# Two transformer blocks on one core: the mLSTM heads, the out products and one norm in another order

## The reference

```python
def mlstm_mixer(x, norm_g, w_in, b_gates, h_norm_g, w_out):
    u = rmsnorm(x, norm_g) @ w_in
    q, k, v, o, gi, gf = jnp.split(u, M_SPLITS, axis=-1)      # 4 heads, dqk 128, dv 256
    ...
    h = mlstm_chunkwise(q, k, v, i_pre, f_pre)
    h = rmsnorm(h, h_norm_g.reshape(M_HEADS, M_DV))...        # a mean of squares per head
    h = h * jax.nn.sigmoid(o.astype(jnp.float32))             # the output gate
    return h.astype(x.dtype) @ w_out

# per head: s = (q k^T) * exp(dmat - m);  num = s v;  den = sum(s)
#           h = num / max(|den|, exp(-m))
# moba_mixer: 8 heads of 128; causal softmax over the 256 tokens; then o @ w_o
# conv_ffn:   rmsnorm, @ w_up (5632 wide), 3-tap causal convolution, silu(gate) * val, @ w_down
```

## Time and profile before

| what | us |
|---|---|
| median of 3 runs (lowest, highest) | 1027.2 (1026.81, 1027.39) |
| the profiled execution: its own time | 1025.42 |
| its span, first to last instruction | 1023.6 |
| PE busy (share of the span) | 987.5 (96%) |
| DVE busy | 632.9 (62%) |
| ACT busy | 274.1 (27%) |

### The profile page before, as it was taken

One profiled execution on the slowest core, in us unless ns is written; L12 is line 12 of the kernel. 1 busy time (PEld: TensorE's weight loads), 2 busy tenths in 40 slices (PEclk: granted clock), 3 DMA queues, 4 the chain that ended last, 5 costly groups with the idle time before them and its releaser, 6 DMA issues.

```text
span 1023.6 us, 15183 instructions
## 1 busy us (share of the span) xinstructions
PE 987.5 (96%) x5811; PEld 882.9 (86%) x5811; DVE 632.9 (62%) x1400; ACT 274.1 (27%) x602; POOL 1.1 (0%) x8
## 2 busy tenths in 40 slices
PE   6999899999999999999999999999999989999987
PEld 5788588999999988888899999999888878888876
DVE  2302437878778571254287867875799951799843
ACT  1111301121121122244022111112433553623651
POOL 0000000000000000000000000000000000000000
PEclk9999999999999999999999999999999999999999
DMA  8991036577577292450537767754733035443001
GB/s 254 354 354 48 1 124 185 188 265 267 204 260 255 80 336 76 144 185 1 156 109 257 269 200 258 275 191 133 223 124 127 26 104 178 151 130 122 21 1 41
DMA packets 132100, 170.80 MB, mean 167 GB/s; under 512 B 8643, under 2 KB 119251, under 8 KB 131923
## 3 DMA queue, kind: packets, MB, share of 16 engines
q1 hardware_dynamic: 127856, 167.33, 49.9%
q10 hardware_dynamic: 4195, 2.81, 0.9%
HBM read 168.93 MB, written 2.64 MB: 168 GB/s over the span
## 4 chain that ended last, share of the span: by engine, by line
PE 84%; DVE 11%; ACT 2%; issue 1%; DMA 1%; ACTq 0%; DVEq 0%
PE bank L1093 24%; PE bank L1106 15%; PE bank L897 14%; PE bank L908 9%; PE bank L1371 5%; DVE work L1920 4%; PE bank L1069 3%; PE bank L1255 2%; PE bank L1358 2%; PE bank L1274 2%; PE bank L1214 1%; PE bank L1297 1%; DVE fring L1995 1%; PE bank L915 1%; DMA ring<-in_a_w_in 1%
## 5 line engine op out<-in xcount | busy, mean ns | idle before, releaser
L1106 PE MATMUL bank<-work,fring 128*128 128x256 f32 x704 | 155.6, 379 | 0.0
L1106 PEld LDWEIGHTS bank<-work,fring 128*128 128x128 f32 x704 | 132.1, 190 | 17.0
L897 PE MATMUL bank<-xg,ring 128*128 128x256 f32 x576 | 127.6, 381 | 3.7 <-DVE xg L1654 2.0
L897 PEld LDWEIGHTS bank<-xg,ring 128*128 128x128 f32 x576 | 108.5, 190 | 21.4 <-issue 4.6
L1755 DVE SCALAR_TENSOR_TENSOR work<-work,cols 128x256 f32<-128x256 f32 x176 | 71.6, 480 | 53.2 <-ACT work L620 53.2
L1920 DVE SCALAR_TENSOR_TENSOR work<-work,cols 128x256 f32<-128x256 f32 x240 | 99.1, 481 | 1.2 <-ACT work L779 0.5
L1093 PE MATMUL bank<-sq,fring 128*128 128x128 f32 x640 | 84.5, 275 | 0.0
L620 ACT ACTIVATE work<-work,cols 128x256 f32<-128x256 f32 x88 | 45.6, 589 | 122.2 <-DVE work L1734 100.8
L1093 PE MATMUL bank<-sq,ring 128*128 128x128 f32 x640 | 78.0, 275 | 0.0
L1093 PE MATMUL bank<-ring,fring 128*128 128x128 f32 x640 | 77.9, 275 | 0.0
L1093 PEld LDWEIGHTS bank<-sq,fring 128*128 128x128 f32 x640 | 77.9, 192 | 0.0
(11 more groups left out here) (296 smaller groups left out, 1262.6 us busy)
## 6 DMA issues: line engine op xcount, KB each, us to landing
fring<-in_f_w_up SPq DMA_DIRECT2D x44, 1024.0 KB, 7.6
work<-in_w_ada SPq DMA_DIRECT2D x32, 768.0 KB, 6.3
fring<-in_f_w_down SPq DMA_DIRECT2D x22, 1024.0 KB, 5.0
ring<-in_w_in SPq DMA_DIRECT2D x18, 1024.0 KB, 6.0
ring<-in_a_w_in SPq DMA_DIRECT2D x12, 1024.0 KB, 12.0
ring<-in_w_kv SPq DMA_DIRECT2D x8, 1024.0 KB, 5.4
ring<-in_w_out SPq DMA_DIRECT2D x8, 1024.0 KB, 5.2
ring<-in_a_w_out SPq DMA_DIRECT2D x4, 1024.0 KB, 11.1
```

The lines of the kernel that those rows point to most:

```text
L897: last = mm(bank[:, T * c:T * (c + 1)], w[:, k, at + P * c:at + P * (c + 1)], x[:, k, :], start=(k == 0), stop=(k == nk - 1))
L1106: last = mm(pb[m // 2][:, T * (m % 2):T * (m % 2 + 1)], w[:, k, P * m:P * (m + 1)], f_act[:, par, T * k:T * (k + 1)], start=(first and k = ...
```

## The change

It does the following, all in `first_block`:

- mLSTM heads, VectorE: the probabilities of heads 1, 2 and 3 are issued ahead of the square sums of heads 0, 1 and 2; ScalarE issues the decays of the next heads ahead of the numerators.
- mLSTM heads, TensorE: the gate projections 10 and 11 leave the loop over the heads. They run behind it, in halves (`gate_product`), into banks 2 and 3, with the square sum of head 3 between the halves of the first, and the spreads in the middle of the second half of the other. VectorE scales gate 2 inside the root's chain, and gate 3 between the heads' final products.
- `m_y` moves to the memory of `m_q` and `m_k`. VectorE scales a head (`m_scaled`) before it has gated the one ahead (`m_gated`). Projection 12 runs by pairs of input chunks, both output chunks for each pair.
- `gained(1, ...)` writes a pair of chunks of `xg` right behind each `add_pair`.
- `residual_norm(2)` is issued ahead of `gained(2, a_xq, ...)`.
- MoBA: pieces 0 and 1 of `values` run at n = 0, pieces 2 to 7 at n = 1 to 6. Projection 28 runs by input chunk (`heads_out`), two, three and one heads at n = 7, 8 and 9, and the last two behind the loop. ScalarE issues `rows_out` at n = 3 and 7, ahead of the exponentials.

```diff
--- before.py
+++ after.py
@@ -177,7 +177,8 @@
         m_pt = [W(9472 + 384 * i, 9856 + 384 * i) for i in range(2)]
-        m_y = xg
+        m_y = three(W(0, 2048), DC)
+        M_O_BANK = (7, 7, 2, 3)
         m_sqn = sq[:, 0:4, :]
@@ -593,9 +594,11 @@
             decay(0)
-            for h in range(4):
-                if h < 3:
-                    decay(h + 1)
+            decay(1)
+            numer(0)
+            decay(2)
+            decay(3)
+            for h in range(1, 4):
                 numer(h)
@@ -685,6 +688,8 @@
                 for n in range(10):
+                    if gate is not None:
+                        gate(n)
                     if n < 8:
@@ -694,8 +699,6 @@
                                 .then_inc(S("exp_done"), 1)
-                    if gate is not None:
-                        gate(n)
                     if 1 <= n < 9:
@@ -708,8 +711,8 @@
             def values_out(n):
-                if n in (4, 8):
-                    rows_out(9 + n // 4)
+                if n in (3, 7):
+                    rows_out(9 + (n + 1) // 4)
 
@@ -1008,10 +1011,10 @@
                     pe.wait_ge(S("m_v_out"), 8)
-                if h < 3:
+                if h < 2:
                     if h > 0:
                         pe.wait_ge(S("m_o_scaled"), h)
-                    feat(8 + h, pb[7], xg)
+                    feat(8 + h, pb[M_O_BANK[h]], xg)
                 pe.wait_ge(S("m_p"), h + 1)
@@ -1030,16 +1033,36 @@
                     m_square_sum(h - 1)
+            def gate_product(h, c, ks):
+                for k in ks:
+                    last = mm(pb[M_O_BANK[h]][:, T * c:T * (c + 1)], slot8(8 + h)[:, k, P * c:P * (c + 1)], xg[:, k, :],
+                              start=(k == 0), stop=(k == DC - 1))
+                return last
+            arrived(pe, 10)
+            gate_product(2, 0, range(DC))
             m_square_sum(3)
-            pe.wait_ge(S("m_o_scaled"), 3)
-            feat(11, pb[7], xg)
+            gate_product(2, 1, range(DC)).then_inc(S("product"), 1)
+            arrived(pe, 11)
+            gate_product(3, 0, range(DC))
+            gate_product(3, 1, range(4))
             pe.wait_ge(S("rstd_done"), 2)
...
                 spread(h, rows[0:4, 7, :], "f_spread")
+            gate_product(3, 1, range(4, DC)).then_inc(S("product"), 1)
             pe.wait_ge(S("m_num_out"), 8)
-            for m in range(4):
-                feat(12 + m, pb[m], m_y,
-                     x_ready=(lambda k: pe.wait_ge(S("m_y_done"), k // 2 + 1)) if m == 0 else None)
+            arrived(pe, 12)
+            for pair in range(4):
+                pe.wait_ge(S("m_y_done"), pair + 1)
+                for c in range(2):
+                    for k in (2 * pair, 2 * pair + 1):
+                        last = mm(pb[0][:, T * c:T * (c + 1)], slot8(12)[:, k, P * c:P * (c + 1)], m_y[:, k, :],
+                                  start=(k == 0 and c == 0), stop=(k == DC - 1), skip_group_check=True)
+            last.then_inc(S("product"), 1)
+            for m in range(1, 4):
+                feat(12 + m, pb[m], m_y)
 
@@ -1161,6 +1184,7 @@
                         h = 8 * a + n - 2
+                        pe.wait_ge(S("tok_out"), 2 * (9 + (n - 2) // 2))
                         pe.wait_ge(S("pt_out"), h + 1)
@@ -1203,28 +1227,39 @@
 
-                if n < 8:
-                    i, b, half = n // 4, n // 2 % 2, n % 2
-                    if n == 0:
-                        arrived(pe, 26)
-                        pe.wait_ge(S("turn_out"), 3)
-                    if n == 4:
+                if n == 0:
+                    arrived(pe, 26)
+                    pe.wait_ge(S("turn_out"), 3)
+                for q in ((0, 1) if n == 0 else (n + 1,) if n < 7 else ()):
+                    i, b, half = q // 4, q // 2 % 2, q % 2
+                    if q == 4:
                         arrived(pe, 27)
...
                                   skip_group_check=True)
-                    if n % 4 == 3:
+                    if q % 4 == 3:
                         last.then_inc(S("product"), 1)
...
                     pe.wait_ge(S("turn_out"), 8)
-                if n >= 2:
-                    pe.wait_ge(S("tok_out"), 2 * (9 + (n - 2) // 2))
+                if n == 7:
+                    arrived(pe, 28)
+                    pe.wait_ge(S("max_done"), 7)
+                if n >= 7:
+                    heads_out(((0, 1), (2, 3, 4), (5,))[n - 7])
+            def heads_out(ks):
+                for k in ks:
+                    pe.wait_ge(S("o_out"), k + 1)
+                    for c in range(2):
+                        last = mm(pb[0][:, T * c:T * (c + 1)], slot8(28)[:, k, P * c:P * (c + 1)], a_oT[:, k, :],
+                                  start=(k == 0 and c == 0), stop=(k == DC - 1), skip_group_check=True)
+                return last
 
             attention(0, a_qT, lambda h: a_kT[:, h, :], lambda b, h: a_v[:, b, A_DH * h:A_DH * (h + 1)], values)
-            for m in range(4):
-                if m == 0:
-                    pe.wait_ge(S("o_out"), 8)
+            heads_out((6, 7)).then_inc(S("product"), 1)
+            for m in range(1, 4):
                 feat(28 + m, pb[m], a_oT)
@@ -1605,25 +1640,37 @@
                 product(dve, 8 + h)
-                v.tensor_tensor(m_o[:, 2 * h:2 * h + 2, :], three(pb[7][:, :], 2), rbc2, ALU.mult)\
+                v.tensor_tensor(m_o[:, 2 * h:2 * h + 2, :], three(pb[M_O_BANK[h]][:, :], 2), rbc2, ALU.mult)\
                     .then_inc(S("m_o_scaled"), 1)
...
             m_decay(1)
-            for h in range(M_HEADS):
+            def m_probs(h):
                 dve.wait_ge(S("m_exp"), 2 * h + 2)
...
                     .then_inc(S("m_p"), 1)
-                if h < 2:
-                    m_decay(h + 2)
-                if h < 3:
-                    m_output_gate(h)
+            def m_squares(h):
                 dve.wait_ge(S("m_num_out"), 2 * h + 2)
...
                 v.tensor_tensor(x[:, 0, :], x[:, 0, :], x[:, 1, :], ALU.add).then_inc(S("m_sqs"), 1)
+            m_probs(0)
+            m_decay(2)
+            m_probs(1)
+            m_output_gate(0)
+            m_squares(0)
+            m_decay(3)
+            m_probs(2)
+            m_output_gate(1)
+            m_probs(3)
+            for h in range(1, 4):
+                m_squares(h)
 
@@ -1637,29 +1684,41 @@
             dve.wait_ge(S("ms_done"), 1)
+            m_output_gate(2)
             dve.wait_ge(S("guess_done"), 2)
...
             newton(1, a, y, t, by=r1)
-            m_output_gate(3)
-            for h in range(M_HEADS):
+            def m_scaled(h):
                 dve.wait_ge(S("f_spread"), h // 2 + 1)
...
                 src = pb[4 + h // 2][:, T * (h % 2):T * (h % 2 + 1)].unsqueeze(1).broadcast_to([P, 2, T])
-                then(v.tensor_tensor(x, x, src, ALU.mult))
+                return link(v.tensor_tensor(x, x, src, ALU.mult))
+            def m_gated(h, scaled):
+                after(scaled)
                 dve.wait_ge(S("m_o_gate"), h + 1)
-                product(dve, 11)
-                for i in range(2):
-                    c = 2 * h + i
+                for c in (2 * h, 2 * h + 1):
                     ins = v.scalar_tensor_tensor(m_y[:, c, :], m_num[:, c, :], col("a_h_norm", c), m_o[:, c, :],
...
                 ins.then_inc(S("m_y_done"), 1)
-            product(dve, 11)
+            first, second = m_scaled(0), m_scaled(1)
+            m_gated(0, first)
+            third = m_scaled(2)
+            m_gated(1, second)
+            fourth = m_scaled(3)
+            m_gated(2, third)
+            m_output_gate(3)
+            m_gated(3, fourth)
             s_forms(1, 1)
...
                 add_pair(m, pb[m])
-            gained(1, xg, "f_norm", "xg_ready")
+                gained(1, xg, "f_norm", "xg_ready", pairs=[m])
 
@@ -1817,8 +1876,8 @@
 
+            residual_norm(2)
             gained(2, a_xq, "b_norm", "xq_ready")
-            residual_norm(2)
             mean_square(3, pb[7][:, 0:T], ms[:, 0:T], D)
```

## The result

| | before | changed |
|---|---|---|
| median of 4 runs each, us | 1027.01 (1026.57 to 1027.39) | 1013.75 (1013.48 to 1015.70) |
| ratio of the two, 95% interval | | 0.9873 (0.986 to 0.9887) |
| profiled execution: own time, span | 1025.42, 1023.6 | 1013.48, 1011.7 |

The same comparison was measured twice more and gave 0.9880 (0.9863 to 0.9897) and 0.9874 (0.9857 to 0.9890).

A forecast was written before the change was run, and what follows sets the result against it. PE's work plus its standing still was taken to bound the kernel. Savings of 7.8 + 1.2 + 2.8 = 11.8 us take the median from 1027.2 to 1015.4 us, 8-in-10 range 1014.0 to 1018.2.

The forecast's parts named there:

- mLSTM tail, 7.8 us: mLSTM heads to first MLP matmul: 57.32 us hold 49.51 of work, so 7.8 us saved, range 5.4 to 7.9.
- the root: Root chain in the mLSTM tail: ready at 116.2, PE reaches the spreads at 117.33, margin 1.1 us.
- Switches between pieces: Cost of changing between short matmul groups: taken as 0, at most 0.9 us on some 10 switches.
- Norm, 1.2 us: Norm issued ahead of the query input: square sum starts straight behind its projection, 1.2 us saved, bounds 1.0 to 1.3.
- MoBA, 2.8 us: MoBA heads: of 3.21 us idle 0.4 stays, 2.8 us saved, bounds 2.1 to 3.2.
- The wait for the first probabilities: MoBA heads, from scores to transposes: 3.46 us against 3.03 of work, so a wait of 0.4 us stays.
- Given back: Whether later stretches lose the gain: MLP loads move with PE, the second block shifts whole, so nothing is lost.
- rivals B to F: Late mLSTM waits 16%, late MoBA copies 6%, half given back 5%, exposed weight loads 3%, gaps only missing trace records 2%.
- E: Short interleaved groups expose weight loads, 0.19 us for each of 192 records, 36 us: slower, 1051 us; chance 3%.
- B: New waits in the mLSTM tail replace the old, returning up to 2.5 of the 7.8 us: 1017.9 us; chance 16%.
- The granted clock is 1.00 there, the upper of the two levels, so gaps cost only themselves: In the stretches touched, clock at its upper level, so closing a gap saves only the gap's length.
- the saving applies to both: The 11.8 us come off both the profiled execution (1025.42 to 1013.6) and the median (1027.2 to 1015.4).

The follow-up runs named there:

- spreads_last_c: Changed kernel with the four spreads behind the whole of gate 3 instead of in the middle of its second half: median 1018.79 us.
- out_by_chunk: Changed kernel with projection 12 by output chunk (output chunk outermost) instead of by pairs of input chunks: median 1017.33 us.
- p3_moba: Kernel before with only the MoBA part of the change: median 1024.72 us, ratio 0.9975.
- warm_start: Changed kernel with 4 more matmuls of ones by ones, results unread, in the wait for the first weights: median 1012.39 us.
- after_c: Changed kernel as it is, profiled a third time: median 1013.90 us, ratio to before 0.9874.

## Why the prediction was right or wrong

- **mLSTM tail, 7.8 us:** 7.57, and 0.08 in the first MLP, where a restart went. Right in every wait: no wait at the heads, the root with a margin of 1.45 (1.1 forecast), the last head 0.6 early (0.7), `xg` in time. The 0.2 missing are a net figure. Switches between pieces, which I set to nothing, take 0.5: the first 16 records of L1040 take 3.65 us to the next start, where 16 x 0.216 = 3.46 fill them, the next 40 take 8.83 for 8.64, and the 8 behind the spreads 1.83 for 1.73. The square sums and the spreads take 0.2 less than I had put down.
- **Norm, 1.2 us:** 1.21.
- **MoBA, 2.8 us:** 2.96. The wait for the first probabilities is 0.32 with its drain, not 0.4; another 0.1 is the restart behind the old wait ahead of the out projection, for which I had no term.
- **Given back:** nothing. MLP 1 and 2 and the keys are the same within 0.1 us. Layer 2 takes 149.23 to 149.30 in the changed kernel and 149.0 to 149.7 before, by where the fall ahead of it ends; the means agree to 0.1.
- The rivals B to F did not happen. E (weight loads exposed by short groups) is refuted by L1040 and L1256: 40 records in 8.83 us and 12 in 2.59 us from start to start, thus still 0.22 each. The rule that the prediction puts beside it, from the Trainium skill ("TensorE: Matmul & The Clock Gate", Part 2), comes out in its favourable case here too, with full 128-row loads at 0.22 us a record. B was priced too low: the waits that its own part lists, 0.34 + 0.93 + 1.9, come to 3.2 us and not 2.5, so 1018.6, outside the range that was to take it in.

**What failed is the step "The granted clock is 1.00 there, the upper of the two levels, so gaps cost only themselves", and with it "the saving applies to both".** The earlier trace rows have no stretch of the mLSTM tail; the same table over 99.16 to 156.48 us gives 1.00 too, but that is one execution, in which the clock happened not to fall there. In the other three unfilled profiles of the old order it did fall behind the spreads. The mean of the four tails is (57.84 + 58.20 + 58.17 + 59.00) / 4 = 58.30, so the tail is worth 8.0 us and not 7.6. And layer 1 of the second block, which no edit touches, takes 149.47 in the mean of the same four and 148.50 in the three of the changed kernel: another 1.0. Together: 8.0 + 0.08 + 1.21 + 0.08 + 2.96 + 1.0 = 13.3 us. Measured, over all executions, are 13.3 us between the medians (1027.09 in 74 of before, 1013.83 in 13 of the changed kernel) and 13.0 between the means (12.3 to 13.6, an estimate of the 95% interval from the scatter of the executions). That the sum meets the medians to the last digit is luck, for it rests on four and three profiles that scatter by more than 1 us. With all profiles that have no filling between the layers, five of the old order and ten of the new, layer 1 takes 149.4 against 148.9, which is worth 0.5 us and makes the sum 12.9. So the term of the clock is 1.0 to 1.4 us, and 11.8 is outside what was measured.

The 11.9 us between the first two profiles were a coincidence of two things: the execution of before had its fall in layer 1 (0.9 us, and 0.2 in layer 2), and that of the changed kernel a start 1.0 us longer. The fixed part is 7.57 + 0.08 + 1.21 + 0.08 + 2.96 = 11.9 us.

So the sum of the waits was right to 0.1 us (11.8 against 11.9; its parts were off by 0.2 and less, in both directions), and the missing term is the clock, 0.5 us in the tail and 0.5 to 1.0 us in layer 1. That idle time right beside the spreads, ahead of them or behind, lets it fall is shown: it fell in five of six profiles with such idle time (four of five of the old order, and spreads_last_c, which differs from the changed kernel by the place of the spreads alone), and in none of the 12 in which full-width matmuls stand straight on both sides. Waits further behind did not do it: out_by_chunk waits twice, 0.7 and 1.4 us, from 16 records behind its spreads on, and its clock stays up there.

Open is why the clock falls in layer 1 with the old order in five of five and with the new in three of ten, though the wait ahead is the same 2.88 us in all; and why filling three of the gaps of the old order raised the clock in part of the executions only: its spreads are still preceded by 0.34 us of waiting and stand next to the filled gap. Filling all of them, with no gap around the spreads, was not tried.

## What to carry to other kernels

Where PE bounds, lay the same matmuls end to end stretch by stretch and subtract; with start-to-start times from one trace each part came out to 0.2 us. Then look at the granted clock behind every gap in more than one profile, and at the mean clock of the timed executions beside that of the profiled one (here 0.998 against 0.992 to 0.997): a gap of 1 to 3 us can be followed by 3 to 7 us at half clock, in some executions only, and that belongs to the range. Work that needs nothing (here half a gate projection) is best kept for both sides of a chain that runs through other engines, not spent before it.

## What I had not expected of the hardware

- The lower clock stays for 3.4 us (changed kernel, from 12.8 us) or about 7 us (p3_moba at 127 to 134, warm_start at 859 to 866, spreads_last_c at 124 to 131).
- It falls in some executions and not in others behind the same wait of 2.88 us between the layers. At the start the first 64 records run at the upper pace in five profiles (waits of 1.71 to 1.90 us ahead) and partly at the lower in ten (1.72 to 2.15 us).
- The clock column of a profile can read 1.00 at its start while the records come at half pace (after_c at 14 us: 4 in 1 us against 7).
- A change in the first block went with a change in how often the clock falls some 700 us later: in five profiles of five with the old order, in three of ten with the new.
